# Four groups of idle products on TensorE are left out of a fused two-model forward kernel

## What is computed

```python
def first_block(x, ...):
    h = x
    for layer in range(DEPTH):                       # 2
        hn = rms_norm(h, mix_norm[layer])
        mix = hybrid_mixer(hn, ...) if layer % 2 == 0 else conformer_conv(hn, ...)
        h = h + mix
        h = h + swiglu(rms_norm(h, ffn_norm[layer]), ...)
    return h

def stick_breaking_mixer(q, k, v, g_q, g_k):         # part of hybrid_mixer
    z = qh @ kh^T
    log_keep = where(past, log_sigmoid(-z), 0)
    between = reverse_cumsum(log_keep) - log_keep
    w = where(past, exp(log_sigmoid(z) + between), 0)
    out = w @ vh
```

## Time and profile before

| | |
|---|---|
| median of 3 runs | 1031.27 us (1031.12 to 1032.37) |
| profiled execution | 1029.78 us |
| its span | 1028.0 us |
| TensorE busy | 1006.3 us, 98% |
| VectorE busy | 690.8 us, 67% |
| ScalarE busy | 511.2 us, 50% |
| mean DMA rate | 182 GB/s |

### The profile page before, as it was taken

How to read it: one execution, slowest core, us unless ns; L and a number is a source line. 1 busy time by engine, 2 the same in 40 slices (tenths; PEclk the granted TensorE clock), 3 DMA queues, 4 the chain that set the end, 5 groups by cost and what they waited for, 6 DMA issues and landing times.

```text
span 1028.0 us, 15979 instructions
## 1 busy us (share of the span) xinstructions
PE 1006.3 (98%) x6802; PEld 873.5 (85%) x6808; DVE 690.8 (67%) x767; ACT 511.2 (50%) x593; POOL 69.8 (7%) x88
## 2 busy tenths in 40 slices
PE   9999899999999999999999999999999999999997
PEld 6997788888888977988888888889878888888886
DVE  5565478676767766768777667164688876656664
ACT  6567564343436434744444345354677454343444
POOL 0000100000000000001010100000148000000000
PEclk9999999999999999999999999999999999999999
DMA  7642357767665663357888875424000345655551
GB/s 261 225 164 83 130 203 272 237 231 239 222 225 173 222 180 118 126 197 276 301 284 277 291 261 185 170 86 161 1 1 2 145 144 189 206 199 184 183 198 48
DMA packets 33756, 187.60 MB, mean 182 GB/s; under 512 B 3744, under 2 KB 7584, under 8 KB 15136
## 3 DMA queue, kind: packets, MB, share of 16 engines
q1 hardware_dynamic: 25344, 154.82, 43.5%
q0 software_dynamic: 7344, 27.79, 7.6%
q10 hardware_dynamic: 1008, 4.13, 1.1%
HBM read 181.61 MB, written 1.05 MB: 178 GB/s over the span
## 4 chain that ended last, share of the span: by engine, by line
PE 88%; DVE 5%; ACT 3%; DMA 2%; issue 1%; SPq 0%; DVEq 0%; ACTq 0%
PE PS L611 11%; PE PS L613 11%; PE PS L612 11%; PE PS L293 10%; PE PS L294 10%; PE PS L295 10%; PE PS L1199 2%; PE PS L676 2%; PE PS L678 2%; PE PS L677 2%; DMA raw<-wstream 2%; PE PS L644 1%; PE PS L1434 1%; DVE w_lo L280 1%; PE PS L343 1%
## 5 line engine op out<-in xcount | busy, mean ns | idle before, releaser
L280 DVE TENSOR_TENSOR w_lo<-raw,w_hi 128x2048 fp32r<-128x2048 f32 x138 | 316.1, 2291 | 181.2 <-ACT w_hi L276 158.5
L276 ACT ACTIVATE w_hi<-raw 128x2048 fp32r<-128x2048 f32 x129 | 246.4, 1911 | 126.7 <-DMA raw<-wstream 68.5
L611 PE MATMUL PS<-w_hi,a_hi 128*128 128x512 f32 x512 | 203.0, 396 | 0.0
L613 PE MATMUL PS<-w_hi,a_lo 128*128 128x512 f32 x512 | 199.8, 390 | 0.0
L612 PE MATMUL PS<-w_lo,a_hi 128*128 128x512 f32 x512 | 199.7, 390 | 0.0
L293 PE MATMUL PS<-a_hi,w_hi 128*128 128x256 f32 (+1 forms) x512 | 154.8, 302 | 0.4 <-DVE a_lo L479 0.4
L294 PE MATMUL PS<-a_lo,w_hi 128*128 128x256 f32 (+1 forms) x512 | 151.6, 296 | 0.0
L295 PE MATMUL PS<-a_hi,w_lo 128*128 128x256 f32 (+1 forms) x512 | 151.6, 296 | 0.0
L613 PEld LDWEIGHTS PS<-w_hi,a_lo 128*128 128x128 f32 x512 | 96.1, 188 | 20.7
L611 PEld LDWEIGHTS PS<-w_hi,a_hi 128*128 128x128 f32 x512 | 96.3, 188 | 18.8 <-DVE w_lo L280 0.2
L612 PEld LDWEIGHTS PS<-w_lo,a_hi 128*128 128x128 f32 x512 | 96.4, 188 | 18.4
(11 more groups left out here) (398 smaller groups left out, 1446.1 us busy)
## 6 DMA issues: line engine op xcount, KB each, us to landing
raw<-wstream SPq DMA_DIRECT2D x141, 1024.0 KB, 4.9
modraw<-wmod POOLq DMA_DIRECT2D x48, 512.0 KB, 4.4
U<-CU SPq DMA_DIRECT2D x28, 142.0 KB, 2.8
cst<-cst ACTq DMA_DIRECT2D x1, 1632.0 KB, 9.6
mlw<-mlw ACTq DMA_DIRECT2D x1, 1280.0 KB, 5.7
X<-xT SPq DMA_DIRECT2D x2, 512.0 KB, 5.3
raw<-wstream SPq DMA_DIRECT2D x2, 512.0 KB, 8.0
CROW<-crow POOLq DMA_DIRECT2D x1, 1024.0 KB, 5.3
```

Of the source, the lines that this page charges most:

```text
L276: nc.scalar.activation(w_hi[:, slot, :], raw[:, rslot, :], ACT.Copy).then_inc(S("hi_done"), 1)
L280: dve.tensor_tensor(w_lo[:, slot, :], raw[:, rslot, :], w_hi[:, slot, :].bitcast(F32), ALU.subtract).then_inc(S("lo_done"), 1)
L611: nc.tensor.matmul(out, a_hi[:, k, src, ts], wh, start=k == 0, stop=False, skip_group_check=True)
L613: i = nc.tensor.matmul(out, a_lo[:, k, src, ts], wh, start=False, stop=k == KT - 1, skip_group_check=True)
```

## The change

The function and its four calls are deleted. Nothing else is touched; the zeros at L735 and L1498 stay.

```diff
-        def idle_products(bank, n):
-
-            for _ in range(n):
-                nc.tensor.matmul(PS[:, bank, :], zero[:, 0:P], zero, start=True, stop=True)
...
             pe.wait_ge(S("memset_done"), 1)
-            idle_products(2, 10)
             pe.wait_ge(S("memset_done"), 5)
...
             sb_z(0)
             sb_z(1)
             qk_ss(3)
-            idle_products(7, 10)
             sb_between(0)
...
             ctx_sums(pe)
-            idle_products(0, 4)
             out_units_pe(pe, U_PW2, "cv", 2, 1)
             ffn_pe(pe, 1, "ffn1", 3, 4)
-            idle_products(7, 8)
```

## The result

The changed kernel takes 1032.65 us in the median of 22 runs (1030.88 to 1037.32), the kernel before 1031.22 in as many (1029.36 to 1032.41). The ratio is 1.0020 with a 95% interval of 1.0013 to 1.0027: slower, by 1.43 us between the medians and by 2.07 between the means (1033.11 and 1031.04). The forecast for the median was 1032.6.

A forecast was written before the change was run, and what follows sets the result against it. The kernel was taken as a stream of TensorE products, 98 per cent busy. Terms 0 + 0 + 0 + 1.3 us, added to the median 1031.27, gave 1032.6 us; range 1030.9 to 1037.0.

The forecast's parts named there:

- The sum's one term, the start: Without the group at L992, L996 runs at 1.2 GHz and the stream begins at 12.0 instead of 10.66: 1.3 us late.
- the narrow products: Rival at the start: L996's 16-column products may do less for the clock than zeros; 2.0 to 4.8 us, chance 0.10.
- an all-slow start: Bound at the start: the clock stays low for all 16 pieces of L996, which end at 12.67: 2.0 us.
- In that stretch no wait is listed that could take up the delay: From the stream's start to 90 us TensorE is always busy, so 1.3 us at the start is 1.3 at the end.
- The cover of the late groups and of L1170: Idle time follows the groups at L1237, L1240 and L1170, so removing them saves 0; holes become 1.25, 2.17 and 2.95 us.
- I take 0 here, since 2.57 is the nearest row: The new 2.95 us hole before L1133 costs 0, as the existing hole of 2.57 us did nothing.
- The first pair of L1133 takes 0.91 us behind it ... so the clock of the engine was the same: Behind the 2.57 us hole ending at 106.64, the pair takes as long as behind the short hole: clock still higher.
- The argument from the end of the span: The clock held some 4.7 us after the last product ended; 2.95 us is less, against a fall at 93.6 us.
- The holes of 2.17 and 1.25 us ... I give them no case of their own: Holes at L1240 and L1237 are shorter than one that did nothing, so no clock fall was priced there.
- The rival's price: Clock falls in the hole at 93.6 us: 2.0 us for one round, 6.0 for three, 8.8 at most; chance 0.16.
- The 1.49 us between the profiled execution and the median: The profiled execution, 1029.78 us, lies this far under the three-run median, 1031.27; the difference was carried over to the forecast.

The follow-up runs named there:

- the first experiment: Only the group of zero products at the start (L992) left out of the kernel before: median 1031.26 us, ratio 0.9999 (0.9991 to 1.0008).

## Why the prediction was right, and where it wasn't

*The sum's one term, the start: right in the mechanism, high in the size.* 1.3 us were worked out, with bounds of 0 and 4.8. The traced delay is 1.54 us in the changed kernel, but in the three other traces without the group the first products come at 11.14 to 11.26, 0.5 to 1.0 us behind the 10.22 to 10.66 of the traces with it. The fastest runs of the kernels say 1.1 to 1.8: 1030.9, 1030.5, 1030.2 and 1030.6 without the group, 1029.1 with it. The 5.5 us that the prediction took from one execution scatter: by the spacing of the loads the clock rose some 3 to 5.6 us after the first product in the ten traces with the group, and 3.8 to 6.0 us after it in the four without, so nothing shows that the narrow products do less for the clock than the zeros. In the changed kernel's trace the rise was so late that 15 of the 16 pieces ran slowly. The Trainium skill (TensorE: Matmul & The Clock Gate, "Part 1: The HAM clock gate") says that the moment of the rise varies from run to run. The traces agree. One bound was mis-sized: 16 steps of 0.43 us were counted for an all-slow start, but the first two loads go out together, so there are 14, and this trace, slow almost to the end, shows 1.54 us and not 2.0.

*"In that stretch no wait is listed that could take up the delay": wrong in general.* It was true of the one trace that I had. Of the ten traces with the start group six have a wait for KTOK at L1084, of 0.3 to 1.1 us, the second trace of the kernel before among them; the four without the group have none. ScalarE's L1649 starts at 64.4 to 66.3 us with the group and at 64.9 to 65.9 without, so it doesn't follow the start. In those six traces KTOK was ready at 66.0 to 66.9 us, and without the start group TensorE starts L1084 at 66.4 to 67.5: with a KTOK as late as that, little of the delay would be left to pay. Three of the four traces without the group reach the first sb_between at 97.03 to 97.15 us, no later than several of those with it (96.11 to 97.53). This is a likely reason why the median of the first experiment shows no price; no run tests it by itself.

*The cover of the late groups and of L1170: right.* The three holes came out at 1.25, 2.17 and 2.94 us, and taking the groups out shortened nothing: where the clock stayed up, the stage has 51.31 us with and without the group at L1170, and from the zeros of L735 to the input projection there are 484.71 us without the late groups and 484.73 with them.

*"I take 0 here, since 2.57 is the nearest row": this step failed.* It rested on one execution, and put at nothing a fall that costs 1.37 us where it comes alone. The hole at L1170 is open in four traces, and the clock fell in three. The hole of 2.57 us is open in eight, and it fell in three; it did nothing in the one that I had. *"The first pair of L1133 takes 0.91 us behind it ... so the clock of the engine was the same"* was no evidence either: in the three traces where the clock fell behind that hole, the first pair took 0.91, 0.91 and 0.99 us, and what followed took the loss. The argument from the end of the span, that the clock holds for 4.7 us after the last product, failed too: in the changed kernel the clock fell 1.9 us after the last product's end (95.12 to 97.00).

*"The holes of 2.17 and 1.25 us ... I give them no case of their own": wrong for 2.17.* It is open in five traces, and two show a fall, which cost 1.37 and 1.64 us. Behind the hole of 1.25 us there was none in the same five.

*The rival's price: the size was in its range, the shape not.* I had 2.0 for one round and 6.0 for three, up to 8.8. A fall cost 1.3 to 1.6 us where it was alone and 3.2 to 3.4 for two in the stage, because the clock was back before the second round and fell again only within the third (in the changed kernel back at 103.8, the second round from 104.57, the next fall at 110.7). A round at the low clock took 3.8 us instead of 2.0.

*The median: right, partly by luck.* The forecast had 1.3 us for the start and nothing for the clock; the 1.43 us that came are less of the start and some of the clock. The kernel before isn't free of falls itself. Of its 97 runs the 35 with a mean clock of 0.999 or more have a median of 1029.93 us, the 44 at 0.998 one of 1031.37, the 18 below that 1032.48. The changed kernel has 5, 1 and 16 of 22, with 1030.99 us for the first, 1.06 above the same class before. (A mean of 0.998 can come from an early fall behind the last product as well, so that the 44 are not all falls in the body.) The 1.49 us between the profiled execution and the median, which I only carried over, fit this difference; no trace of the kernel before shows it.

*What stays open.* How the 2.07 us between the means divide. Start, L1170 and late groups left out alone give ratios of 0.9999, 1.0003 and 1.0003, all three together 1.0020; but the upper ends of the three intervals are 0.8, 1.2 and 1.5 us, so parts that add up aren't excluded. Putting back either the start or the group at L1170 brings back all of it, by the best values, and why either is enough wasn't tested. In the first experiment more runs have a mean clock of 0.999 or more than in the kernel before (8 of 12 against 13 of 35), which may hide some of the start's price too; but the other pairs show no such help from leaving the start group out (5 of 22 against 3 of 11, 3 of 11 against 4 of 12, 9 of 11 against 21 of 23), so it may be chance.

## What to carry to other kernels

In this kernel products of zeros in a hole of TensorE cost nothing as long as the hole outlasted them, and what they buy is only the clock; so their worth can't be read from the path, nor from one trace: look at several executions with their granted clocks. The places where such a group did something here are ahead of work that would otherwise begin at 1.2 GHz, and in holes of over 2 us. A late start costs its delay only where no later wait takes it up, and one trace can miss such a wait. All four groups together are worth 0.2 per cent of this kernel.

## What the runs showed of the hardware that wasn't expected

The same hole, with the same instructions around it, lets the clock fall in one execution and not in the next: 2.95 us with no fall in one trace, 2.17 us with a fall in another. The fall may come inside the hole (97.0 in the changed kernel) or up to 1.4 us after TensorE has resumed (108.5 with the group at L1170 put back). Of the eight low stretches in the bodies of the traces six lasted 3.4 us and two 6.8. The granted clock of the profile doesn't show the start: it reads 1.00 there while products step at the pace of 1.2 GHz.
